# One load of expert weights is issued ahead of the first gathered rows in a hybrid attention and mixture-of-experts block

## What is computed

```
def hier_moe(h, w_rg, b_rg, w_re, b_re, w_gate, w_up, w_down):
    t = h.reshape(B * S, D)
    g_prob = jax.nn.softmax((t @ w_rg + b_rg).astype(f32), axis=-1)
    g_idx = jnp.argmax(g_prob, axis=-1)
    ...
    top_p, top_e = lax.top_k(e_prob, TOP_K_EXPERTS)
    ...
    for e in range(N_EXPERTS):
        hid = jax.nn.silu(t @ w_gate[e]) * (t @ w_up[e])
        y = y + gates[:, e:e + 1] * (hid @ w_down[e]).astype(f32)
```

## Time and profile before

| | us |
|---|---|
| median of 3 runs | 1267.99 |
| lowest and highest run | 1262.97 and 1271.01 |
| profiled execution | 1260.54 |
| its span, first to last instruction | 1258.7 |

### The profile page before, as it was taken

How to read it: one execution, slowest core, us unless ns; L and a number is a source line. 1 busy time by engine, 2 the same in 40 slices (tenths; PEclk the granted TensorE clock), 3 DMA queues, 4 the chain that set the end, 5 groups by cost and what they waited for, 6 DMA issues and landing times.

```text
span 1258.7 us, 13952 instructions
## 1 busy us (share of the span) xinstructions
PE 1082.9 (86%) x5506; PEld 695.9 (55%) x5506; DVE 431.1 (34%) x783; ACT 327.9 (26%) x571; POOL 293.1 (23%) x195
## 2 busy tenths in 40 slices
PE   3999999999999999889999559987878878778881
PEld 2778899777789888768867413322222222222220
DVE  3222594488870232359982710000000000000003
ACT  5343642333332544452231301111011011011000
POOL 4332243432224433374440210000000000000002
PEclk8999999999999999999989769999898989889996
DMA  6222223312224522243354749999999999999965
GB/s 155 67 68 67 68 68 101 84 51 67 67 56 146 166 68 68 67 151 100 100 234 200 218 164 402 409 412 419 414 411 418 419 413 415 404 405 412 424 269 207
DMA packets 124455, 278.63 MB, mean 221 GB/s; under 512 B 11561, under 2 KB 97593, under 8 KB 108025
## 3 DMA queue, kind: packets, MB, share of 16 engines
q1 hardware_dynamic: 114168, 254.15, 54.8%
q0 software_dynamic: 4992, 13.37, 3.1%
q10 hardware_dynamic: 5248, 10.49, 2.2%
HBM read 265.45 MB, written 14.63 MB: 223 GB/s over the span
## 4 chain that ended last, share of the span: by engine, by line
PE 60%; DMA 27%; DVE 5%; issue 2%; ACT 2%; POOL 2%; SPq 1%; POOLq 0%; ACTq 0%; DVEq 0%
DMA arena<-w_exp_up_in 25%; PE bank L451 15%; PE bank L472 13%; PE bank L783 10%; PE bank L689 6%; PE bank L746 3%; PE bank L796 2%; DVE work L1239 2%; PE bank L519 1%; PE bank L630 1%; PE bank L587 1%; PE bank L647 1%; POOL piece_r L1614 1%; PE bank L576 1%; DVE piece_r L1348 1%
## 5 line engine op out<-in xcount | busy, mean ns | idle before, releaser
L783 PE MATMUL bank<-arena,work 128*64 128x512 f32 x1024 | 253.7, 653 | 62.5 <-DMA arena<-w_exp_up_in 61.6
L1588 POOL TENSOR_TENSOR piece_r<-arena,piece_r 128x1024 fp32r<-128x1024 f32 x84 | 202.0, 2413 | 384.6 <-ACT piece_r L864 384.6
L451 PE MATMUL bank<-piece_r 128*128 128x512 f32 x960 | 238.0, 399 | 0.0
L783 PEld LDWEIGHTS bank<-arena,work 128*64 128x64 f32 x1024 | 78.8, 150 | 235.3 <-issue 229.2
L451 PEld LDWEIGHTS bank<-piece_r 128*128 128x128 f32 x960 | 175.5, 188 | 41.8 <-issue 7.4
L1502 DVE TENSOR_TENSOR work<-work,bank 128x256 f32<-128x256 f32 x32 | 13.5, 422 | 455.6 <-ACT work L1089 455.6
L472 PEld LDWEIGHTS bank<-piece_r 128*128 128x128 f32 x1344 | 162.1, 192 | 7.4 <-issue 7.4
L472 PE MATMUL bank<-piece_r 128*128 128x256 f32 x1344 | 165.4, 284 | 0.0
L796 PE MATMUL bank<-arena,work 128*64 128x512 f32 x512 | 116.9, 598 | 15.2 <-ACT work L1091 14.7
L864 ACT ACTIVATE piece_r<-arena 128x1024 fp32r<-128x1024 f32 x84 | 88.6, 1057 | 145.1 <-DMA arena<-w_in_in 81.9
L1646 POOL DMA_INDIRECT arena<-h_rows,idx_all x32 | 29.6, 926 | 405.5 <-PE bank L775 402.7
(11 more groups left out here) (230 smaller groups left out, 940.3 us busy)
## 6 DMA issues: line engine op xcount, KB each, us to landing
arena<-w_exp_gate_in SPq DMA_DIRECT2D x32, 2048.0 KB, 31.5
arena<-w_exp_up_in SPq DMA_DIRECT2D x32, 2048.0 KB, 37.9
arena<-w_exp_down_in SPq DMA_DIRECT2D x32, 2048.0 KB, 38.9
arena<-w_in_in SPq DMA_DIRECT2D x68, 512.0 KB, 3.9
y_rows<-work ACTq DMA_DIRECT2D x64, 96.0 KB, 7.6
arena<-w_branch_gla_in SPq DMA_DIRECT2D x8, 512.0 KB, 3.9
arena<-w_branch_dsa_in SPq DMA_DIRECT2D x8, 512.0 KB, 5.1
arena<-w_out_in SPq DMA_DIRECT2D x2, 2048.0 KB, 8.6
```

The lines of the kernel that those rows point to most:

```text
L451: last = mm(bank[n % 2][:, :], w[:, k, :], h[:, k, :], start=(i == 0 and k == 0), stop=(i == 2 and k == K - 1))
L783: last = mm(bank[0][hf * WIDE:(hf + 1) * WIDE, :], hTe[sl][:, k, :], wgu[sl][2][:, :, k, hf * HALF:(hf + 1) * HALF], start=(k == 0), stop= ...
L1588: Q.tensor_tensor(quarter(w_lo, q), quarter(w_raw, q), quarter(w_hi, q).bitcast(F32), ALU.subtract).then_inc(s["wlo_ready"], 1)
```

## The change

One wait of SP is removed. The load of expert 2's down matrix is issued directly behind the loads of expert 2's gate and up matrices, and no longer after the rows of expert 0 have been gathered. Nothing is added, and no other engine's stream changes.

More of the change, by code:

```diff
@@ L406, in _ @@
             load_up(2, 2)
-            sp.wait_ge(xg_loaded[0], 16)
             load_down(2, 2)
```

## The result

The changed kernel is slower by a little: 1267.5 us against 1263.5 us, medians of 20 runs each. The ratio is 1.0031 with a 95% interval of 1.0016 to 1.0046, so the change costs 4 us (2 to 6). This is within 1% of no change and clear of zero.

The account below looks back on a forecast made before the run. The expert stage was taken as bound by the full DMA stream, hence by its start. Terms 0 (what leaves), 0 (clock and first product) and +2 (scatters later) on 1268.0 gave 1270.0 us, range 1263 to 1280.

Parts of the forecast that it names:

- The frame: Whole expert stage: the end moves as much as the transfer stream's start, which hangs on scatters, table, gather, transposes, first product.
- Taking 2.1 MB out of the stretch behind the first gather: DMA after the first gather: gain 0, since a pause follows and the loop's first load stays tied; at most 5.1 us.
- The term that isn't 0: Scatters on the path: they meet the earlier load and land later, +2 us, bounds 0 and 5.1.
- the count of 12 small packets against 12 data packets of 0.32 us: Each DMA engine, queues in turn: small packets spread over 3.8 us instead of about 2, last scatter about 1.8 us later.
- one repetition: Scatters beside the load: one more jam of a scatter pair, +6 us; chance 0.20 shared with the load-first case.
- rival 3: Scatters beside the load: the jam repeats, 5.9 us per pair, up to +22 with a slow gather; from two repetitions 0.12.
- base: Whole kernel before the change: 1268.0 us, the median of the runs shown, to which the forecast added 2.
- Rival 1: Scatters' landing: set by their own small writes, the load fills half-empty DMA engines, change 0, 1268 us; chance 0.25.
- Rival 2: Scatters' landing: their count fills only after all the loads land, +5, 1273 us; chance 0.20 shared with one repetition.
- Rival 4: First product and gathers: quicker without the load beside them, at most 1.9 us, 1266 us; chance 0.05.
- account of that product by the clock: Expert 0's first product: 3.8 us at half clock speed cost 1.9 us, leaving nothing for the load beside it.

Follow-up runs that it names:

- second execution of either kernel: One more profiled execution each of the changed kernel and the kernel before, nothing else changed: 1268.5 and 1268.4 us.
- the one with the load beside the table load: Against the kernel before, expert 2's down load is issued once all scatters have landed, not after the first gather: 1268.20 us against 1262.07, ratio 1.0051.
- the one with the unread products: Kernel before plus 14 products that nobody reads, in PE's idle time ahead of the first gathered rows: 1261.27 us against 1263.17, ratio 1.0007.
- the kernel with eight transfers: Changed kernel with expert 2's down matrix loaded by eight transfers with 1 KB runs; against the kernel before, 1266.16 us to 1263.17, ratio 1.0031.

## Why the prediction held, and where its steps were off

**The frame was right.** The end of the kernel moved with the start of the stream, and the start hung on scatters, table, gather and first product. From the loop's first load to the end of the span it was 509.9 us before and 511.1 us after, and 509.5 us in the second execution of either kernel. Taking 2.1 MB out of the stretch behind the first gather won nothing, as was forecast: the pause of the DMA engines grew instead.

**The term that isn't 0 was mis-sized.** The scatters' wait was to grow by 2 us. It grew by 3.5 us (6.53 to 10.08), and between the second executions by 4.4 (5.62 to 10.01); the table load added 0.1 to 0.6 us. The chain as a whole grew by 4.6 and 5.4 us. The step that failed is the count of 12 small packets against 12 data packets of 0.32 us. Its picture fits the changed kernel, where the two queues went out in nearly equal numbers, but it took 0.32 us for each data packet, and in the jam of 728 to 732 only 34 of them went out in 4 us. This second breakdown is the one repetition of rival 3, which was priced at +6. Counted from the last scatter, the last small packet went out 7.2 us later, and not 1.8. The prediction also let the release follow the last packet at the old distance, and this distance shrank by 3.7 us. That the two errors nearly cancel is luck: the truth lay between the forecast and one repetition, at the edge of the first (+1 to +4) and within the range.

**The total was helped by its base.** 1270.0 was forecast and 1267.5 measured. But the base of 1268.0 came from three runs, and over 20 runs the kernel before takes 1263.5. The base was 4.5 us too high and the term 2 us too low. The step from one kernel to the other was forecast at half its size.

**Rival 1** (hidden entirely) is refuted by the ratio's interval, and by the wait of 1.4 to 1.9 us in the quiet: the small writes by themselves are not slow. What had spoken for it is real all the same. The silence between the last small packet and the release is 3.7 to 4.5 us in the four profiles in which the scatters met the loads of the kernel before (both of that kernel, the one with the load beside the table load, the one with the unread products) and 0.6 to 0.9 us in the nine others, quiet ones and those with more loads alike. In those four most of the packets of the last six scatters went out in a burst of 2 us as the loads ran dry. It makes up 3.7 of the 5 us that the kernel before pays. Why it stands there is open.

**Rival 2** (the load goes first, to the last packet) gave +5, near what the chain shows, for a reason that the changed kernel's trace contradicts: the count was full at 733.9 and the load landed at 735.8. The Trainium skill (DMA: Bandwidth & Descriptors, "Queues, rings and completion order") has a semaphore's increment wait for earlier writes of its DMA engine. This can have held it up for those packets of the load that had gone out before, but not for the whole load. The same section's turn-taking between packets agrees with the nearly equal counts of q0 and q1 in the changed kernel (148 and 128, 34 and 34), but not with the 684 and 112 of the kernel with eight transfers; and it doesn't tell how long a turn lasts in a jam.

**Rival 4** (a quicker first product without the load beside it) is refuted: 10.03 and 9.79 us without the load, 8.98 and 9.35 with it. The prediction's account of that product by the clock was right for the one execution, but its length varies by about 1.4 us from one execution to the next, which the prediction did not see.

**What the prediction missed** is that the kernel before pays the same price already. It read the 86 GB/s over 720 to 724 as a trouble of the loads, and took the 6.5 us of POOL's wait as given, where only 1.4 to 1.9 of it were the scatters' own. The change that pays is in the other direction: to hold back more, not less.

**What stays open** is why the traffic of the whole core falls to 70 to 90 GB/s for some four us when 4-byte scatters run beside loads, and why the release then comes 4 us behind the last small packet in one case and 0.6 us behind it in the other. That scatters and loads are both needed is shown: quiet scatters flow, and in the kernel before the loads with ACT's store of the rows beside them ran at 412 GB/s over 712 to 716, before the first small packet. It is also shown that smaller packets of the load don't cure the cost of the chain. The read of the table pays as well. Its 5.9 us fit plain queueing behind 2.1 MB, which are 5.1 us at 414 GB/s, but no run tells this from other causes. The mechanism inside the DMA engines was not tried.

## What to carry to other kernels

When a chain of small dependent transfers (scatter, table, gather) is on the path, look at what else is in flight beside it: here the scatters paid 4 to 5 us and the table load 4 us for bulk loads that were in no hurry. Issue ahead only as many bytes as land before the chain begins, hold the rest until its last step has landed, and make sure that what is held back fits into the next pause of the stream. Removing a wait on a load is no gain where the freed stretch ends in a pause that is tied to something else.

## What the runs showed of the hardware

A read of 6 KB landed in 1.9 us in the quiet and in 5.9 us when 2.1 MB had been issued 0.3 us ahead of it on another queue. Eight scatters of 128 4-byte writes let POOL go 1.4 to 1.9 us after the last one when no load was in flight, 5.4 to 6.5 us beside the tail of 6.3 MB, 7.4 us with 7.3 MB and 10.0 us with 8.4 MB (7.4 and 9.8 us where the last 2.1 MB went in packets of 2 KB and of 1 KB). Beside the tail of 6.3 MB POOL's release came 3.7 to 4.5 us behind the last of the small packets, with the DMA engines empty, and in every other case 0.6 to 0.9 us behind it. The granted clock of TensorE came back from 0.50 (1.2 GHz) to 1.00 (2.4 GHz) at no fixed distance from PE's restart, so that the same 32 products took between 8.6 and 10.0 us. In the experiment with the filler in the kernel before it was 1.00 over 728 to 732 and 0.50 again over 736 to 740, with 4.6 us of idle PE between.
